# An RWKV-7 mixer phase: streams announced before the bonus, K masks on ScalarE and GpSimd, outputs of one half ahead of the scan, weights loaded by projection

## The reference, cut to what matters

```python
def wkv_scan(r, w, k, v, kk, a, s0, reverse):
    ...
    def step(S, inp):
        r_t, w_t, k_t, v_t, kk_t, a_t = inp
        sa = jnp.einsum("bhvk,bhk->bhv", S, kk_t)
        S = (S * w_t[:, :, None, :]
             - sa[..., None] * (kk_t * a_t)[:, :, None, :]
             + v_t[..., None] * k_t[:, :, None, :])
        return S, jnp.einsum("bhvk,bhk->bhv", S, r_t)
...
def rwkv7_readout(o, streams, r_k, gn_g, gn_b, w_out, out_dtype):
    ...
    y = ((o - mean) * lax.rsqrt(var + GN_EPS)).reshape(B, T, RW_WIDTH) * gn_g + gn_b
    bonus = jnp.sum(jnp.sum(r[:, :, None] * kd * r_k, axis=-1, keepdims=True) * v[:, :, None], axis=2)
    y = (y + bonus.reshape(B, T, RW_WIDTH)) * jax.nn.silu(g)
    return y.astype(out_dtype) @ w_out
```

## Time and profile before

| | us |
|---|---|
| median of 3 runs | 4436.56 |
| lowest and highest | 4434.79, 4439.36 |
| the profiled execution, its time | 4434.42 |
| its span on the core | 4432.6 |
| PE busy in the span | 4138.8 (93%) |
| DVE, ACT, POOL busy | 2434.7, 1593.8, 96.0 |

### The profile page before, as it was taken

One profiled execution on the slowest core, in us unless ns is written; L12 is line 12 of the kernel. 1 busy time (PEld: TensorE's weight loads), 2 busy tenths in 40 slices (PEclk: granted clock), 3 DMA queues, 4 the chain that ended last, 5 costly groups with the idle time before them and its releaser, 6 DMA issues. The chain is left out here.

```text
span 4432.6 us, 90840 instructions
## 1 busy us (share of the span) xinstructions
PE 4138.8 (93%) x40018; PEld 3526.6 (80%) x40018; DVE 2434.7 (55%) x3825; ACT 1593.8 (36%) x2833; POOL 96.0 (2%) x83
## 2 busy tenths in 40 slices
PE   6999999999889999799998988999989999888998
PEld 4667666676667777699998667999989999657998
DVE  3555554555322333375665455766666566556777
ACT  3323223323124444353333333433343333334443
POOL 0000000000000000000000030000000000020000
PEclk9999999999899999899999999999999999999999
DMA  3000000001533443311212111121212211211232
GB/s 149 23 23 23 22 22 3 23 23 40 219 138 147 168 172 134 114 67 58 77 67 80 39 46 39 67 77 67 77 39 77 77 67 60 78 55 58 97 114 77
DMA packets 42601, 332.17 MB, mean 75 GB/s; under 512 B 4193, under 2 KB 8674, under 8 KB 12898
## 3 DMA queue, kind: packets, MB, share of 16 engines
q1 hardware_dynamic: 42210, 326.37, 20.3%
HBM read 324.26 MB, written 2.10 MB: 74 GB/s over the span
## 5 line engine op out<-in xcount | busy, mean ns | idle before, releaser
L837 PE MATMUL banks<-x_hi,w_hi 128*128 128x384 f32 (+1 forms) x2496 | 807.9, 324 | 26.1 <-DVE x_lo L1111 22.2
L838 PE MATMUL banks<-x_lo,w_hi 128*128 128x384 f32 (+1 forms) x2496 | 805.3, 323 | 0.0
L839 PE MATMUL banks<-x_hi,w_lo 128*128 128x384 f32 (+1 forms) x2496 | 805.0, 323 | 0.0
L923 ACT CAST w_hi<-landing_all 128x512 fp32r<-128x512 f32 x768 | 457.5, 619 | 326.7 <-DVE landing_all L1022 300.1
L1014 DVE TENSOR_TENSOR w_lo<-landing_all,w_hi 128x512 fp32r<-128x512 f32 x768 | 516.0, 684 | 50.6 <-ACT w_hi L923 50.6
L837 PEld LDWEIGHTS banks<-x_hi,w_hi 128*128 128x128 f32 x2496 | 474.0, 190 | 30.4 <-DVE x_lo L1111 23.4
L838 PEld LDWEIGHTS banks<-x_lo,w_hi 128*128 128x128 f32 x2496 | 474.2, 190 | 0.3
L839 PEld LDWEIGHTS banks<-x_hi,w_lo 128*128 128x128 f32 x2496 | 473.8, 190 | 0.0
L837 PE MATMUL banks<-g_hi,w_hi 128*128 128x384 f32 (+1 forms) x1232 | 421.3, 342 | 0.0
L838 PE MATMUL banks<-g_lo,w_hi 128*128 128x384 f32 (+1 forms) x1232 | 421.3, 342 | 0.0
L839 PE MATMUL banks<-g_hi,w_lo 128*128 128x384 f32 (+1 forms) x1232 | 421.2, 342 | 0.0
(11 more groups left out here) (437 smaller groups left out, 6602.8 us busy)
## 6 DMA issues: line engine op xcount, KB each, us to landing
landing_all<-in_w SPq DMA_DIRECT2D x132, 1024.0 KB, 4.9
arena_first<-in_ada_w SPq DMA_DIRECT2D x44, 2048.0 KB, 8.2
weight_ring_first<-in_rw_pair SPq DMA_DIRECT2D x8, 2048.0 KB, 8.5
weight_ring_first<-in_da_head SPq DMA_DIRECT2D x8, 2048.0 KB, 12.7
landing_all<-in_w_in SPq DMA_DIRECT2D x12, 1024.0 KB, 4.9
weight_ring_first<-in_ada_w SPq DMA_DIRECT2D x4, 2048.0 KB, 10.9
landing_all<-in_w_out SPq DMA_DIRECT2D x8, 1024.0 KB, 4.9
x_res<-in_x_t SPq DMA_DIRECT2D x2, 2048.0 KB, 12.8
```

The costliest lines, as they stand in the source:

```text
L837: mm(o, wh, xh, start=first, stop=False, skip_group_check=onto)
L838: mm(o, wh, xl, start=False, stop=False, skip_group_check=onto)
L839: return mm(o, wl, xh, start=False, stop=last, skip_group_check=onto)
L923: nc.scalar.copy(SH[:, q % RING], raw(q)).then_inc(whi.h, 1)
```

## The change

Six edits, all for this phase:

1. `streams` is announced by the last bb instruction; the bonus announces a signal of its own, `bonus_taken`. TensorE starts `first_products` of half 0 after `streams`, and waits for `bonus_taken` ahead of half 1, whose products overwrite banks 6 and 7.
2. The K products go to banks 4e and 4e+1, the B products to 4e+2 and 4e+3, for every j. So each group with j = 1 or 2 waits until both of the group before it in its half have been taken.
3. VectorE takes the B products alone. ScalarE copies the K products unmasked into MK (6 copies a pair, ahead of its As copies, `mk_copied`).
4. GpSimd multiplies MK with `mask_kb` in place (6 instructions a pair, `mk_masked`), ahead of its two sums. `g_products` waits for `mk_masked`.
5. `scan_of` waits for half 0's `block_ready`, draws three pieces of `fill` (the half 0 outputs of blocks 0 to 2), keeps their cost as credit, and only then waits for half 1's.
6. The weights of a pair are loaded as four DMAs of 128 columns (rows of 512 bytes), each once the same projection of the pair before is done, with a signal each; the first pair's too.

```diff
@@ first phase, SyncE
-                sp.dma_start(W_pair, self.dram["rw_pair"][0]).then_inc(pair_w.h, 16)
+                for ready, col in zip(pair_w, (1, 0, 2, 3)):
+                    sp.dma_start(W_pair[:, :, col * P:col * P + P], self.dram["rw_pair"][0][:, :, col * P:col * P + P]).then_inc(ready.h, 16)
...
@@ SyncE
+                    for j in range(4 if i else 0):
+                        c = columns_of[j] * P
+                        sp.wait_ge(proj_done.h, proj_done.at(i - 1, j + 1))
+                        sp.dma_start(Wp[:, :, c:c + P], self.dram["rw_pair"][i][:, :, c:c + P]).then_inc(w_ready[j].h, 16)
                     if i:
-                        sp.wait_ge(proj_done.h, proj_done.at(i, 0))
-                        sp.dma_start(Wp, self.dram["rw_pair"][i]).then_inc(w_ready.h, 16)
                         sp.wait_ge(lora_done.h, lora_done.at(i, 0))
...
@@ GpSimd
+                    for j in range(3):
+                        for e in range(2):
+                            raw = MK[e][:, j].rearrange("p h d w n -> p h (d w n)")
+                            pool.wait_ge(mk_copied.h, mk_copied.at(i, 2 * j + e + 1))
+                            nc.gpsimd.tensor_tensor(raw, raw, mask_kb.unsqueeze(1).broadcast_to([P, 2, 256]), ALU.mult).then_inc(mk_masked.h, 1)
                     for e in range(2):
-                        pool.wait_ge(am_masked.h, am_masked.at(i, 5 + e))
+                        pool.wait_ge(mk_masked.h, mk_masked.at(i, 5 + e))
...
@@ TensorE
-                    ba = am_bank(e, j)
                     for q in range(4):
-                        d, src, col = q % 2, (kb, bb)[q // 2], 128 * q
+                        d, src, ba, col = q % 2, (kb, bb)[q // 2], 4 * e + 2 * (q // 2), 128 * (q % 2)
...
-                            if j == 2:
-                                pe.wait_ge(am_masked.h, am_masked.at(i, e + 1))
+                            if j:
+                                pe.wait_ge(am_masked.h, am_masked.at(i, 2 * (j - 1) + e + 1))
+                                pe.wait_ge(mk_copied.h, mk_copied.at(i, 2 * (j - 1) + e + 1))
+                            elif e:
+                                pe.wait_ge(bon_ready.h, bon_ready.at(i, 1))
                             first_products(i, e, j)
                     for e in range(2):
-                        pe.wait_ge(am_masked.h, am_masked.at(i, 2 + e + 1))
+                        pe.wait_ge(am_masked.h, am_masked.at(i, 4 + e + 1))
                         inverse_seed(i, e)
...
+                                pe.wait_ge(mk_masked.h, mk_masked.at(i, 5 + e))
                                 g_products(i, e)
...
                 def scan_of(i, fill):
+                    pe.wait_ge(block_ready.h, block_ready.at(i, 1))
+                    owed = -sum(next(fill) for _ in range(3))
                     pe.wait_ge(block_ready.h, block_ready.at(i, 2))
-                    owed = 0
...
@@ ScalarE, at the head of blocks_of
+                    for j in range(3):
+                        for e in range(2):
+                            act.wait_ge(am_done.h, am_done.at(i, 4 * (2 * j + e) + 4))
+                            nc.scalar.copy(MK[e][:, j].rearrange("p h d w n -> p h (d w n)"), banks2(4 * e)[:, :, 0:256]).then_inc(mk_copied.h, 1)
...
@@ VectorE
-                    L.mark(tt(bb[:, 1], bb[:, 1], E3[:, 1], ALU.mult))
+                    L.mark(tt(bb[:, 1], bb[:, 1], E3[:, 1], ALU.mult), streams)
...
-                    L(tt(bon[nxt % 2], bank(6, T), v, ALU.mult), streams)
+                    L(tt(bon[nxt % 2], bank(6, T), v, ALU.mult), bon_ready)
...
-                            src = banks2(am_bank(e, j))
-                            L.mark(tt(MK[e][:, j].rearrange("p h d w n -> p h (d w n)"), src[:, :, 0:256], heads(mask_kb), ALU.mult))
-                            L(tt(XR[e][:, j].rearrange("p d w h n -> p h (d w) n"), src[:, :, 256:512].rearrange("p h (x n) -> p h x n", n=CH),
+                            src = banks2(4 * e + 2)
+                            L(tt(XR[e][:, j].rearrange("p d w h n -> p h (d w) n"), src[:, :, 0:256].rearrange("p h (x n) -> p h x n", n=CH),
```

21 lines of the change are left out of this document (14 added, 7 removed).

## The result

| | before | changed |
|---|---|---|
| median of six runs each, us | 4435.68 | 4405.4 |
| the profiled execution, its time | 4434.42 | 4413.05 |
| its span | 4432.6 | 4411.3 |

The ratio is 0.9934, with a 95% interval of 0.9923 to 0.9946: 30.3 us faster, by the medians, where 28 were forecast. The profiled execution of the changed kernel is one of its longer ones (the runs lie between 4397.82 and 4417.71), so the two traces differ by only 21.3 us. One of the ten executions of only_loads, further down, took 8484.55 us at a granted clock of 1.00, for a reason that nothing on record shows; the ratios leave it out.

A forecast was written before the change was run, and what follows sets the result against it. TensorE, busy 93% of the span, was taken as the bound, with only its idle time and clock to win. 15 + 8 + 5 = 28 us off the median of 4436.56 gave 4408 us, range 4397 to 4424.

The forecast's parts named there:

- Part 1: Start of the blocks stage, head sum's end to half 1's first level: 15 us gained over eight pairs (4 to 22).
- clean pair: A pair without issue waits at the blocks stage's start: head sum's end to half 1's first level, 10.4 us against 12.27.
- Rival (e): Blocks stage's start: VectorE's identity add L1920 doubles beside GpSimd's masks (shared interfaces); gain 20 us, time 4416, chance 0.04.
- issue waits: Blocks stage's start: TensorE's instructions arrive late behind weight loads; 0.6 us for seven pairs, 3.0 for the last, 7.2 in all.
- GpSimd's six masks: Blocks stage, ahead of MK's first reader: 6 to 14 us a pair, GpSimd done by 20 us, nothing waits.
- Rival (d): Wait ahead of L1514: masks above 5.0 us make TensorE wait; at 6 us each 48 us, time 4456, chance 0.02.
- Part 2: The scan's start: moved outputs fill TensorE's idle time behind the last transition, 1.0 us a pair, 8 us (5 to 10).
- Part 3: Clock at the scan's start: four of five low spells go, 1.33 us each, 5 us (0 to 6.7).
- Part 4: The split weight loads: later pairs' start earlier, the first pair's delay constants that have 23.9 us to spare; 0 us.
- rival (c): The blocks' levels give the gain back and the clock falls between groups: gain under 8.9 us, 4428 to 4441, chance 0.07.
- (a): TensorE's waits marked issue stay whole despite split loads: gain 10 to 17 us, time 4420 to 4426, chance 0.22.
- (b): Everything works: only the last pair's issue wait left, all five low clock spells gone; 37 us, about 4400, chance 0.15.

The follow-up runs named there:

- only_loads: The kernel before with only its weight loads changed, to four DMAs of 512 KB a pair: 4431.18 us, ratio 0.9989.
- late_masks: The changed kernel with GpSimd's masks held until both halves' identity adds on VectorE are done: 4407.34 us, ratio 0.9930.
- masks_x5: The changed kernel with each of GpSimd's K masks done five times over: 4476.07 us, one run.
- mid_burst: The changed kernel with one weight DMA of 2048 KB a pair, held until the third level's half 0: 4432.81 us, ratio 0.9984.
- one_piece: The changed kernel with one piece of outputs ahead of the first scan step instead of three: 4405.48 us, ratio 0.9953.
- scan_loads: The changed kernel with the last 512 KB of a pair's weights held until the scan stage begins: 4400.01 us, ratio 0.9937.

## Why the prediction was right, step by step

**Part 1, forecast 15 us, measured 14.1.** The clean pair: 10.4 forecast, 10.66 found. Half 1's seed was to come at 7.8 us behind H and came at 394.22 - 385.92 = 8.30. The 0.5 us are the identity add's, 1.53 instead of 0.96. This is the step that failed: I took 0 by the one row in which L1920 had run beside GpSimd. That row was misread, and the price of the wait was put at nothing by it. GpSimd's L1313 had begun 0.05 us *after* L1920, and it was GpSimd's instruction that was long: 1.78 us, where the same sum takes 1.00 in the median of the changed kernel's 16:

```profile
L1327 POOL TENSOR_TENSOR arena_first<-arena_first x16: 992/1002/1717, 135.6 to 1046.0; 128x384 f32<-128x384 f32 x16
```

What the Trainium skill says (GPSIMD Engine Reference, Specifications: shared SBUF interfaces, contention for instructions with two SBUF inputs) holds here, and late_masks shows it; the row had said so too, on the other engine. Rival (e) had the mechanism right and its size too high: +0.35 us in the median of 16, not +0.96, and part of it hidden. The issue waits, taken at 7.2 us, come to 91.07 - 8 x 10.66 = 5.8, within which the last pair's 3.45 us is the 3.0 I had put there:

```profile
1044.76 1.77 PE L1484 MATMUL banks<-arena_first 64*64 64x64 f32 x57 [3.45 <-issue]
```

**GpSimd's six masks**, bounded at 1.04 to 2.37 us each, took 1.27 to 2.01; GpSimd was done 12.6 to 12.8 us behind H, and MK is first read 31.4 to 35.5 behind it (32 forecast). Rival (d)'s place and price are what masks_x5 showed. ScalarE's copy took the 0.59 us assumed:

```profile
L1739 ACT COPY arena_first<-banks x48: 586/587/592, 126.1 to 1040.8; 128x512 f32<-128x512 f32 x48
L1323 POOL TENSOR_TENSOR arena_first<-arena_first,wkv_consts x48: 1267/1282/2008, 126.8 to 1043.1; 128x512 f32<-128x512 f32 x48
```

**Part 2, forecast 8, measured about 7.** The seventh pair, which had the full clock on both sides, went from 71.54 to 70.24: 1.30 us a pair, the full 1.28. Against it stand 19.3 - 15.8 = 3.5 us in the gap, issue waits that weren't there: 8 x 1.3 - 3.5 = 6.9. The prediction had named the cause and taken 2.2 us for it. These waits have no load beside them: the outputs stand right behind the transitions, where TensorE takes its instructions faster than they come (see mid_burst), and edit 6 can't help there.

**Part 3, forecast 5, measured 6.7 less 4.7.** All five low spells at the scan's start are gone (five windows, 72.87 to 70.24 or so, of which 1.3 is Part 2's). one_piece, and the count over all traces given with it, bear the mechanism out. But new ones appeared elsewhere in this execution: in the first pair's scan, which is 70.14 where 69.68 - 1.3 = 68.4 was to be expected, and in the last's, 37.0 where 35.4 - 1.3 = 34.1 was. Among the other kernels with edit 5 the first pair's scan is 68.5 to 68.7 in four and 70.2 to 73.3 in four, and the last's anything from 33.6 to 37.0. What decides on these stays open.

**Part 4, forecast 0, holds** in its own terms. SyncE still waits for TensorE at the end of the block ahead:

```profile
SPq L465 <- PEq L465: 22.9, 1, 22.9
```

It was 23.9. Edit 6's worth is in Part 1, as the prediction had it, and beyond: undone, it costs 5.4 us at the start and 4.7 in the levels, where the sum had nothing.

**What the sum left out.** Levels and transitions are 2.7 + 1.0 us longer than before, rival (c) in small. With the last slice moved away (scan_loads) the levels are 262.5, below the 263.7 of before, so in the change they still pay for the burst at the start. And the rest of the program was 4.8 us shorter behind the last scan in this pair of traces, with no edit there. Together: 14.1 + 6.9 + 2.0 - 3.7 = 19.3, less 2.5 by which the first head sum came later, plus 4.8: 21.6, against 21.3 by the spans. The median's 30.3 is more than the traces account for, as the profiled execution is 7.7 us above its median; which term the other runs did better in can't be read from one profile.

**The rivals.** (a) is refuted in its strong form by the five starts of 10.66 to 10.69, and right in that such waits ate 0.8 to 0.9 of the gap's 1.3 us in three pairs. (b) would have needed the issue waits gone, and a gain of 37 us. scan_loads takes them away at seven starts but not in the transitions and the gap, and its 4400.01 is 27.5 us below the 4427.53 of its chip, not 37. Luck had a part in how near the forecast came. The two traces bear out 21.3 of its 28 us, as the levels and transitions (3.7) and the new low spells (4.7) had no term; that the medians lie 30.3 apart all the same is nothing that the prediction named.

## To carry to other kernels

When an engine that runs thousands of small instructions shows idle time that nothing releases, look at the instruction packets in the DMA records and at what else the DMA moves in that moment; count the instructions in a us, then shift the transfer and see whether the idle time follows. What stays was never the transfer's. A transfer belongs in the stretch where that engine needs the fewest instructions (here the scan), not where its buffer happens to come free. And when two engines run side by side, read the durations of both before calling the pair harmless: here the one that came second paid.
